# Block exits of a two-block transformer kernel: another order of the last squares, the last weight split and the sums

## The reference

```python
def rms_norm(x, g):
    xf = x.astype(jnp.float32)
    xf = xf * lax.rsqrt(jnp.mean(xf * xf, axis=-1, keepdims=True) + RMS_EPS)
    return (xf * g.astype(jnp.float32)).astype(x.dtype)

def second_block(x, c, mod_w, mod_b, norm_pre, norm_post, ...):
    for l in range(DEPTH):
        mod = (jax.nn.silu(c) @ mod_w[l] + mod_b[l]).reshape(bsz, N_SUB, 3, D_MODEL)
        def pre(x_in, i):
            return rms_norm(x_in, norm_pre[l, i]) * (1.0 + mod[:, i, 1]) + mod[:, i, 0]
        def post_add(x_in, y, i, res_w):
            return x_in + res_w * mod[:, i, 2] * rms_norm(y, norm_post[l, i])
        x = post_add(x, swiglu(pre(x, 0), ffn_w_in[l, 0], ffn_w_out[l, 0]), 0, FFN_RES)
        y = token_mixer(pre(x, 1), ...)
        x = post_add(x, y, 1, 1.0)
        x = post_add(x, swiglu(pre(x, 2), ffn_w_in[l, 1], ffn_w_out[l, 1]), 2, FFN_RES)
```

## Time and profile before

| | us |
|---|---|
| median of 3 runs | 3547.52 (3541.67 to 3555.13) |
| profiled execution, its own time | 3553.79 |
| its span | 3552.0 |
| PE busy in the span | 3350.8 (94%) |
| DVE busy | 2011.1 (57%) |
| POOL busy | 1338.6 (38%) |
| ACT busy | 1173.3 (33%) |
| mean granted clock of TensorE | 0.953 of full speed |

### The profile page before, as it was taken

How to read it: one execution, slowest core, us unless ns; L and a number is a source line. 1 busy time by engine, 2 the same in 40 slices (tenths; PEclk the granted TensorE clock), 3 DMA queues, 4 the chain that set the end, 5 groups by cost and what they waited for, 6 DMA issues and landing times. The chain is left out here.

```text
span 3552.0 us, 44582 instructions
## 1 busy us (share of the span) xinstructions
PE 3350.8 (94%) x16330; PEld 2617.2 (74%) x16330; DVE 2011.1 (57%) x2706; ACT 1173.3 (33%) x1792; POOL 1338.6 (38%) x565
## 2 busy tenths in 40 slices
PE   8999999999987999899998999889998999999997
PEld 6657787657775888787676888668887876778886
DVE  3876685877775445994464442244469934654412
ACT  3354323354323223332433222232233324332232
POOL 3302343302323445452153445444464421534453
PEclk9999999999998999998899999989999978999999
DMA  4524473424453323595142332143235841423321
GB/s 131 169 72 125 127 226 92 151 81 127 131 169 105 95 86 90 84 122 86 48 127 61 106 94 82 50 112 96 86 90 89 122 73 49 133 73 98 92 83 63
DMA packets 587985, 363.85 MB, mean 102 GB/s; under 512 B 58146, under 2 KB 537772, under 8 KB 587564
## 3 DMA queue, kind: packets, MB, share of 16 engines
q1 hardware_dynamic: 587444, 361.51, 39.3%
q10 hardware_dynamic: 376, 0.12, 0.0%
HBM read 346.63 MB, written 12.58 MB: 101 GB/s over the span
## 5 line engine op out<-in xcount | busy, mean ns | idle before, releaser
L152 POOL TENSOR_TENSOR w_lo<-w_raw,w_hi 128x1024 fp32r<-128x1024 f32 (+2 forms) x552 | 1330.6, 2416 | 2167.3 <-ACT w_hi L144 2167.3
L158 PE MATMUL bank<-xh,w_lo 128*128 128x512 f32 x2432 | 985.4, 405 | 41.8 <-DVE xl L2357 26.1
L160 PE MATMUL bank<-xh,w_hi 128*128 128x512 f32 x2432 | 965.3, 397 | 0.0
L159 PE MATMUL bank<-xl,w_hi 128*128 128x512 f32 x2432 | 962.5, 396 | 0.0
L144 ACT ACTIVATE w_hi<-w_raw 128x1024 fp32r<-128x1024 f32 (+2 forms) x552 | 565.6, 1028 | 800.9 <-PE bank L160 732.2
L158 PEld LDWEIGHTS bank<-xh,w_lo 128*128 128x128 f32 x2432 | 465.7, 191 | 160.3 <-issue 42.8
L160 PEld LDWEIGHTS bank<-xh,w_hi 128*128 128x128 f32 x2432 | 464.9, 191 | 106.8
L159 PEld LDWEIGHTS bank<-xl,w_hi 128*128 128x128 f32 x2432 | 465.8, 192 | 103.2 <-issue 4.3
L158 PE MATMUL bank<-HH,w_lo 128*128 128x512 f32 x704 | 278.6, 396 | 0.0
L160 PE MATMUL bank<-HH,w_hi 128*128 128x512 f32 x704 | 278.5, 396 | 0.0
L159 PE MATMUL bank<-HL,w_hi 128*128 128x512 f32 x704 | 278.4, 395 | 0.0
(11 more groups left out here) (506 smaller groups left out, 4555.1 us busy)
## 6 DMA issues: line engine op xcount, KB each, us to landing
w_raw<-in_ffn_w_in_dram SPq DMA_DIRECT2D x176, 512.0 KB, 3.8
m_raw_l<-in_mod_w_dram SPq DMA_DIRECT2D x128, 512.0 KB, 5.1
w_raw<-in_w_in_dram SPq DMA_DIRECT2D x80, 512.0 KB, 4.0
w_raw<-in_mix_w_in_dram SPq DMA_DIRECT2D x64, 512.0 KB, 9.2
w_raw<-in_ffn_w_out_dram SPq DMA_DIRECT2D x64, 384.0 KB, 3.5
w_raw<-in_ffn_w_out_dram SPq DMA_DIRECT2D x64, 320.0 KB, 3.2
m_half_l<-in_mod_w_dram SPq DMA_DIRECT2D x32, 256.0 KB, 2.7
w_raw<-in_w_out_dram SPq DMA_DIRECT2D x16, 512.0 KB, 5.0
```

The lines of the kernel that those rows point to most:

```text
L152: nc.gpsimd.tensor_tensor(ring.lo[s][:, 0:width], ring.raw[s][:, 0:width], ring.hi[s][:, 0:width].bitcast(F32), ALU.subtract).then_inc(rin ...
L158: nc.tensor.matmul(out, wl, xh, start=start, stop=False)
L159: nc.tensor.matmul(out, wh, xl, start=False, stop=False)
L160: return nc.tensor.matmul(out, wh, xh, start=False, stop=stop)
```

## The change

- `take_y`: for tile 7 the plain square comes first, then y, then the scaled square. Its signals are split off (`last_square`).
- The split of the last weight (slot 3) on ACT, which stood behind the two roots of exits 0 and 1, now stands ahead of the squares of tile 7.
- `added` of tile 6 is gone from DVE. Instead PE, ahead of the last weight's part of the last product (m = 7, b = 3), sums `tot` and tile 6 directly (`near_sums`), for exits 0 and 2.
- After the product, PE sums the plain square of tile 7 first, then the other two (`last_sums`, now for exit 1 too); DVE waits for the last of them through `cross_ready`.
- In `exit_norm` on DVE, `part(0)` moves in front of the second reciprocal, and `low(k)` in front of `added(k + 1)` and `scaled(k + 1)`.

```diff
+        def near_sums(i):
+
+            for label, x in ([("sq", sqt), ("ysq", ysq), ("ycr", ycr)] if i < 2 else [("sq", sqt)]):
+                out = free(pe, f"{label}{i}")
+                pe.wait_ge(s["y_added"], 5 * (i // 2) + 5)
+                sums(out, tot[label], True, False)
+                if label == "sq":
+                    pe.wait_ge(*taken(i, KT - 2))
+                else:
+                    pe.wait_ge(*((s["y_square"], 7 * i + KT - 1) if label == "ysq" else (s["y_cross"], 8 * i + KT - 1)))
+                sums(out, x[(KT - 2) % 2], False, False)
 
         def last_sums(i):
 
-            pe.wait_ge(s["y_added"], 6 * (i // 2) + 6)
-            for label, x in ([("ysq", ysq), ("ycr", ycr), ("sq", sqt)] if i < 2 else [("sq", sqt)]):
-                sums(free(pe, f"{label}{i}"), tot[label], True, False)
-            for label, x in ([("ysq", ysq), ("ycr", ycr), ("sq", sqt)] if i < 2 else [("sq", sqt)]):
-                if label == "sq":
-                    pe.wait_ge(*taken(i, KT - 1))
-                else:
-                    pe.wait_ge(s["y_square" if label == "ysq" else "y_cross"], 8 * i + KT)
-                last = sums(held(f"{label}{i}"), x[(KT - 1) % 2], False, True)
-            last.then_inc(s["mean_ready"], 1)
+            pe.wait_ge(s["last_square"], i + 1)
+            sums(held(f"sq{i}"), sqt[(KT - 1) % 2], False, True).then_inc(s["mean_ready"], 1)
+            if i < 2:
+                pe.wait_ge(*taken(i, KT - 1))
+                sums(held(f"ysq{i}"), ysq[(KT - 1) % 2], False, True)
+                pe.wait_ge(s["y_cross"], 8 * i + KT)
+                sums(held(f"ycr{i}"), ycr[(KT - 1) % 2], False, True).then_inc(s["cross_ready"], 1)
 ...
         def exit_norm(i):
 
-            if i == 1:
-                out_sums(i, KT - 1)
-            else:
-                last_sums(i)
+            last_sums(i)
 ...
+                    if m == KT - 1 and b == 3:
+                        near_sums(2 * sub)
                     product(bank[m % 2], n, b, CUT[b + 1] - CUT[b], HH, HL, k0=CUT[b], total=FT).then_inc(ring.used, 1)
 ...
             into = m == 0 and i != 1
-            nc.scalar.activation(y[:, m, :], src, ACT.Identity, scale=post_s[:, i, m:m + 1]).then_inc(s["y_scaled"], 1)
+            if m == KT - 1:
+                nc.scalar.activation(sqt[m % 2][:, :], src, ACT.Square).then_inc(s["last_square"], 1)
+            ins = nc.scalar.activation(y[:, m, :], src, ACT.Identity, scale=post_s[:, i, m:m + 1])
 ...
-                for b in range(4 if m < KT - 1 else 3):
+                for b in range(4):
                     hi(n + 4 + b)
 ...
             exit_norm(2 * sub)
-            hi(b_of + 4 * KT + 3)
 ...
             act.wait_ge(ring.used, B_MO + m + 1)
+            if m == KT - 1:
+                hi(B_MO + 4 + m)
             read(take_y(1, m, held(("mo", m))), ("mo", m))
 ...
         exit_norm(1)
-        hi(B_MO + 4 + KT - 1)
 ...
                 a, b = f"ysq{i}", f"ycr{i}"
+                dve.wait_ge(s["cross_ready"], i + 1)
 ...
-                dve.wait_ge(s["pre_std"], i + 1)
-                V.reciprocal(pre_r, pre_r).then_inc(s["root_ready"], 1)
             dve.wait_ge(s["root_spread"], 2 * i + 2)
 ...
             part(0)
+            if i < 2:
+                dve.wait_ge(s["pre_std"], i + 1)
+                V.reciprocal(pre_r, pre_r).then_inc(s["root_ready"], 1)
 ...
                 if k + 1 < KT:
                     part(k + 1)
+                low(i + 1, k)
+                if k + 1 < KT:
                     added(k + 1)
                     scaled(k + 1)
-                low(i + 1, k)
 ...
-                if 0 < m < KT - 1:
+                if 0 < m < KT - 2:
                     added(part, m)
```

More of the change, by code:

```diff
@@ L1482, in second_block @@
              "probs", "turned", "attended", "o_high", "merged", "dve_step", "tables", "pre_std", "post_ready",
-             "scaled", "new_mean", "h_high", "y_added")
+             "scaled", "new_mean", "h_high", "y_added", "last_square", "cross_ready")
     s = {x: sem(x) for x in names}
@@ L1825, in out_sums @@
                 else:
-                    pe.wait_ge(s["y_square" if label == "ysq" else "y_cross"], 8 * i + m + 1)
-                last = sums(out, x[m % 2], m == 0, m == KT - 1)
-            last.then_inc(s["mean_ready" if m == KT - 1 else "sums_taken"], 1)
-        def last_sums(i):
-            pe.wait_ge(s["y_added"], 6 * (i // 2) + 6)
-            for label, x in ([("ysq", ysq), ("ycr", ycr), ("sq", sqt)] if i < 2 else [("sq", sqt)]):
-                sums(free(pe, f"{label}{i}"), tot[label], True, False)
-            for label, x in ([("ysq", ysq), ("ycr", ycr), ("sq", sqt)] if i < 2 else [("sq", sqt)]):
-                if label == "sq":
-                    pe.wait_ge(*taken(i, KT - 1))
-                else:
-                    pe.wait_ge(s["y_square" if label == "ysq" else "y_cross"], 8 * i + KT)
-                last = sums(held(f"{label}{i}"), x[(KT - 1) % 2], False, True)
-            last.then_inc(s["mean_ready"], 1)
+                    pe.wait_ge(*((s["y_square"], 7 * i + m + 1) if label == "ysq" else (s["y_cross"], 8 * i + m + 1)))
@@ new lines, in out_sums @@
+                last = sums(out, x[m % 2], m == 0, False)
+            last.then_inc(s["sums_taken"], 1)
+        def near_sums(i):
[8 more added lines that the diff above has]
+                sums(out, x[(KT - 2) % 2], False, False)
@@ L2063, in take_y @@
             elif i != 1 and m >= 3:
-                act.wait_ge(s["y_added"], 6 * (i // 2) + m - 2)
+                act.wait_ge(s["y_added"], 5 * (i // 2) + m - 2)
             elif m == 0 and i:
@@ L2067, in take_y @@
             into = m == 0 and i != 1
-            nc.scalar.activation(y[:, m, :], src, ACT.Identity, scale=post_s[:, i, m:m + 1]).then_inc(s["y_scaled"], 1)
-            if i < 2:
-                nc.scalar.activation((tot["ysq"] if into else ysq[m % 2])[:, :], src, ACT.Square, scale=post_s[:, i, m:m + 1]).then_inc(s["y_square"], 1)
+            if m == KT - 1:
+                nc.scalar.activation(sqt[m % 2][:, :], src, ACT.Square).then_inc(s["last_square"], 1)
+            ins = nc.scalar.activation(y[:, m, :], src, ACT.Identity, scale=post_s[:, i, m:m + 1])
+            if m == KT - 1 and i == 2:
+                return ins
+            ins.then_inc(s["y_scaled"], 1)
+            if i < 2:
+                ins = nc.scalar.activation((tot["ysq"] if into else ysq[m % 2])[:, :], src, ACT.Square, scale=post_s[:, i, m:m + 1])
+                if m < KT - 1:
+                    ins.then_inc(s["y_square"], 1)
+            if m == KT - 1:
+                return ins
             return nc.scalar.activation((tot["sq"] if into else sqt[m % 2])[:, :], src, ACT.Square)
@@ L2330, in added @@
             V.tensor_tensor(tot["sq"][:, :], tot["sq"][:, :], sqt[m % 2][:, :], ADD).then_inc(s["y_added"], 1)
-            dve.wait_ge(s["y_added"], 6 * (i // 2) + m)
+            dve.wait_ge(s["y_added"], 5 * (i // 2) + m)
         def entry_norm():
```

## The result

| | before | after |
|---|---|---|
| median of 20 runs each, us | 3555.2 (3541.7 to 3560.1) | 3564.6 (3551.3 to 3570.9) |
| ratio to before | | 1.0028 [1.0016, 1.0039] |
| span of the profiled execution | 3552.0 | 3568.8 |
| mean granted clock | 0.953 | 0.951 |
| first plain square of the second block, start | 1076.56 | 1085.29 |

The kernel is slower by 0.28%, which is 10 us [5.7, 13.9]. That is less than the 0.5% by which the forecast set "no measurable change", but its interval leaves out zero. The forecast was 3550 with 3541 to 3558: the time lies outside, and the loss came out larger than the 2.4 us that were forecast.

What follows compares the result with a forecast made beforehand. PE, busy 94% of the span, was taken as the bound. Per pass exit 0 + 0.9, exit 1 + 0.4, exit 2 - 0.1 make 1.2, for two passes 2.4 us on 3547.5: 3550, range 3541 to 3558.

Steps and rivals of the forecast that it cites:

- no measurable change: Whole kernel: time within 0.5%, 17.7 us, of before; chance 0.95.
- the hold by POOL's split: Exits 0 and 1: POOL's split delays DVE's tile 7 product of y and x; first reciprocal at origin + 4.2 us.
- not held: Rival, exits 0 and 1: POOL's split doesn't hold tile 7's product; reciprocal 1.05 us earlier per exit, 3546; chance 0.15.
- full clock: Rival: PE's clock stays full through the exits, both spreads take 1.13 us; - 2.4 us in all, 3545; chance 0.10.
- the stop of PE: Last product of exit 0: summing near tiles inside it makes PE 1.8 us late and moves the origin by that.
- slower rival: Exit 0: tile 6's product of y and x is held too, PE stands 2.9 us longer; 3556; chance 0.12.
- `low` ahead at 0: Restart after exits 0 and 1: PE starts 1.2 us earlier, DVE's steps lengthen to 2.92; net taken as 0.
- the first tile scaled between the roots: Exits 0 and 1, reciprocal to `scaled(0)`: `part(0)` before the second reciprocal gains 0.7 us in exit 0, 1.1 in exit 1.
- exit 2: Exit 2: two groups of sums inside the product + 0.45, square first on ACT - 0.6; root 0.1 us earlier.
- the base: Starting time the forecast added its 2.4 us to: the median of the runs before, 3547.5 us.

Runs made afterwards that it cites:

- e2: The changed kernel with POOL's split of the last weight waiting until DVE finished tile 7's product of y and x in exits 0 and 1; traced only, no own time.
- e1: The changed kernel with the last weight split put back behind the two roots of exits 0 and 1; ratio to before 0.9992 [0.9977, 1.0007].
- e3: The changed kernel with the groups of near sums moved from before the last 15 matmuls to behind the product; ratio to before 1.0019 [1.0002, 1.0037].
- e4: The changed kernel with only the first `low` ahead of the next tile's addition and scaling, the other seven in the old order; traced only, no own time.
- e5: The kernel before with one edit: the last weight split of exits 0 and 1 ahead of the passes over tile 7; traced only, no own time.
- e7: The changed kernel with ACT's plain square of tile 7 last again, PE's order kept as changed; traced only, no own time.
- c0: The changed kernel once more, no edit; ratio to before 1.0021 [1.0005, 1.0038], + 7.5 us.

## Why the prediction was wrong

**Right: the hold by POOL's split.** Its place (exits 0 and 1), its size (reciprocal at + 4.2, measured 4.10 to 4.12) and its cause were as forecast; e2 takes away POOL's part alone and e1 the split, and the reciprocal moves to 3.05 and 2.05. The rival "not held" is out, and so is "full clock": in after all eight spreads of exits 0 and 1 took 1.97 us or more.

**Right: the stop of PE** for the near sums (1.8; 1.94 and 1.86), shown by e3. The slower rival (tile 6 held too) is out: the product of tile 6 took 0.69.

**Right as a sum, by luck in part: `low` ahead at 0.** The restart gained 1.23 us, DVE's longer steps gave it back. The four exits moved by - 0.55, - 0.23, + 0.45 and + 0.32, and e4 shows the mechanism. That they add up to 0 is the luck: after has 23.86 in each, and before has 23.4 to 24.4, by how long the clock stayed at half.

**Wrong: "the first tile scaled between the roots, worth 0.7 in exit 0 and 1.1 in exit 1".** It was worth 0.11 to 0.19. The prediction had worked out this outcome ("with the first spread at half too, `part(0)` waits for it ... and it is 7.0"; measured 6.95) but priced neither exit by it. For exit 0 it took 0.7, the price with the first spread at full clock, although its own row of exit 0 shows that spread at half, 2.05 us. For exit 1 it took the middle of the two better values, because the row of before has the spread at full; what it missed there is that its own other term moves this one: the hold makes the first spread of exit 1 start 5.2 us behind the product instead of 3.8. Both readings also came from the first pass alone. In the second pass of before the first spread of exit 0 took 1.13, and PE's wait in exit 1 was 4.70, not the "about 5.7" of the prediction, since the second spread there took 2.05: which level a spread gets isn't fixed by the exit.

Over the 44 exits 0 and 1 of the eleven traces, all 12 first spreads that began up to 3.8 us behind the origin took 1.13 us; of the four of e2, which began at 4.15 to 4.18, one did; of the 28 that began at 5.18 or later, 24 took the full 2.05 and two 1.13 (exit 0 of the second pass, in before and in e5). The granted clock says the same: it fell 5.6 to 8.6 us behind the origin in those 12 exits, and 2.0 to 5.5 us behind it in 27 of the 28. That the delay is the cause rests on e1 and e2, which change little else ahead of that spread: begun at 3.15 it took 1.13 four times, at 4.15 to 4.18 1.13 to 2.05, at 5.2 in after 1.97 to 2.05. The two exceptions show that the start alone doesn't decide. Between the product and the spread PE does only a few groups of small sums.

In numbers: (0.7 + 1.1) x 2 = 3.6 us of gain forecast, 0.5 measured, which is 3.1 of the 3.8 us that the sum was short.

**Wrong, small: exit 2** at - 0.1; it was + 0.2. Two groups of sums inside the product cost 0.77 (e3), not 0.45, and the square first gave back 0.57 (e7): - 0.57 + 0.77 = + 0.2.

**Wrong: the base.** The forecast was put on the median of 3 runs, 3547.5; over 20 it is 3555.2. The 2.4 us on that base give 3557.6, the 6.2 give 3561.4, and measured is 3564.6. The prediction took in "part of the scatter of the runs of before", but placed its middle at the lower of its two values (the profiled execution, 3553.8, was the other, and it was the better one). This is the larger part of the miss in the number: of the 14.7 us between 3549.9 and 3564.6, 7.7 are the base, 3.8 the exits, and 3.2 are open. On the base of 20 runs the same terms would have given 3557.6.

**Open.** 6.2 us are found in the exits, and the runs give 10 [5.7, 13.9] (c0: 7.5 [1.8, 13.5]); both intervals hold the 6.2, so there may be no difference at all. The distance from exit 0's output to exit 1's origin, code untouched by the change, scatters between 406 and 412 us in the eleven traces, so a part outside the exits can't be excluded, nor shown from profiles.

## What to carry to other kernels

Don't put work that isn't needed yet ahead of a serial chain, even on an engine with room: here a split of 1 us on ACT sent POOL off just so as to lie on DVE's next two-input operation, and the delay then let the matmul clock fall for the two spreads behind it. Price terms of one chain together: when one step makes the chain later, look again at each later step whose price had two values (clock at half or full, held or not), and take the value that goes with the new time. Where a row of the trace already shows which of the two values holds, take that one and not a middle. Where an execution scatters by 15 us outside the changed code, compare distances between events in the changed stretch, and set a forecast on more than three runs.

## What the runs showed of the hardware

**Which of the two begins first is what counts.** DVE's product of y and x (512 columns, 0.69 us alone) begun 0.94 us behind POOL's split took 1.96 us (after); begun 0.45 behind, 2.44 (e5); both ended 0.55 us behind POOL. The residual addition, of the same size, begun 0.16 us ahead of POOL took 0.63 (e1), and POOL 2.66 instead of 2.35. DVE operations with one input in PSUM ran at their usual 0.29 inside POOL's split (e2, 1469.34 and 1469.67), and the first with two inputs in SBUF (1469.99) was held. The Trainium skill, "SBUF — State Buffer", Who interferes with whom, states that a VectorE instruction with two SBUF inputs contends with a GpSimd instruction that reads SBUF, and that the order of issue, not the shape of the operation, decides who is blocked. These rows agree in each of these cases.

**The clock in the gap.** The same eight matmuls took 1.13 us at full and 2.05 at half clock, 0.92 us twice on a chain of some 14. In the changed kernel with its last split at three places, the first of them began 3.15 us behind the product (e1: 1.13 in four exits of four), 4.15 to 4.18 (e2: 1.13, 1.60, 1.63, 2.05) or 5.2 (after: 1.97 to 2.05).

**Small sums inside a product on PE** held it up for longer than their own time: six groups, 0.22 us each in a row, for 1.9 us (e3 against after), of which some 0.2 is the wait for tile 6; two groups for 0.77.
